# First attention reordered around its score units, and full-width meta scores in the second

## The chip, the cores and the metric

The kernel runs on one core of a Trainium2 chip, as one launch. The metric is the device time of the launch in microseconds. Three timed runs of the kernel before gave a median of 2028.56 us (2028.44 to 2029.75).

## What is computed

Two transformer blocks run one after the other in float32 over 512 tokens of width 1024. The first block prepends 16 meta tokens (528 positions) and has two layers; only its first attention and, in one detail, its second are touched here. The first attention is a differential one, with 8 heads:

```python
def diff_attention(q1, q2, k1, k2, v, lam, ...):
    def probs(qb, k):
        s = einsum('bqhd,bkhd->bhqk', qb, k) * scale          # d = 64
        return softmax(where(mask, s, -inf), axis=-1)
    a = probs(qb1, k1) - lam * probs(qb2, k2)                 # two maps
    return einsum('bhqk,bkhd->bqhd', a, v)                    # v: 128 wide

def diff_attn_layer(h, ...):
    q, k, v = split(rms_norm(h, g_norm) @ w_qkv)              # rotary on q and k
    o = diff_attention(...)
    o = rms_norm(o, g_sub) * (1.0 - lam_init)                 # per head, 128 wide
    return h + o.reshape(B, L, H * DIFF_V_DIM) @ w_o
```

The mask is causal by chunks: the meta tokens are chunk 0, the frames follow in chunks of 64. The second attention (`mla_attention`, 16 heads, 64 + 32 wide) has one map for each head. Gated feed-forward layers, a second block and final norms follow; the diff doesn't touch them.

## The kernel before

Activations lie with features on the partitions and tokens along the free side. A projection is three matmul passes for each 128x128 block (`passes`, L805 to L807): high part by high part, low part of the activation, low part of the weight. DMA brings the weights in halves, ScalarE makes the high part (`hi_part`, L2256), GpSimd the low part (L739). Every engine has one hand-written program in order; semaphores join them.

In the first attention each head is cut into five units. Units 0 to 3 are 128 queries against 528, 400, 272 and 144 keys, unit 4 is the 16 meta queries against 16 keys. For a unit TensorE makes the scores of both maps (`scores`, L1090), VectorE clears a corner (L1806) and takes the negative maximum (L1808, `maximum`), ScalarE the exponentials with their sums (`exps`, L2440), VectorE the combination of both maps (`combine`, L1817 to L1824), TensorE transposes it (`transposes`, L1105 and L1109), ScalarE copies it back (`take_transposed`, L2450 and L2452), TensorE multiplies by the values (`values`, L1121 and L1123) and VectorE copies the output (`take_output`, L1829). The scores of units 1 and above reuse the PSUM banks of unit 0 and so wait for its exponentials.

Between these steps of head h TensorE computes head h+1's query, key and value in six pieces (`piece_a`, 24 passes each) into banks 0 and 1; VectorE takes them out (L1786 for the value). The order on TensorE (`head_a`, L1254): scores of units 1 to 4; for each unit its transposes, one piece, its values; with unit 4 the scores of the next head's unit 0 go ahead. At the end come the sum of squares of head h-1's output (`sub_sum`, L877), also in banks 0 and 1, and the transposes of the next value (`value_transposes`, L1132 and L1133). ScalarE makes the inverse root of that sum (`sub_rms`, `inverse_rms`: logarithm L2324, exponential L2326), VectorE scales head h-2's output and splits it (`sub_scale` L1905, `sub_hi` L1911, `sub_lo` L1916) between the units.

Piece 0 waits until the logarithm has read the sum out of banks 0 and 1: in `piece_a`, L1043, `pe.wait_ge(ln_done, N_SUB + summed + 1)`, with `summed` = hd - 2. Heads 0 and 1 are called with `before=False` and lack that wait; head 0 has `sums=False` and no sum of squares.

The last head (`last_head_a`, L1273) has no next projection. Blocks of the output projection (`wo_blocks`, operands `g_hi` and `g_lo`, eight blocks, one for each head) stand between its units; block k can start when head k's output is normalised and split. `tiles(J_WO, ...)` closes the first two tiles with what is left (`tile_pair`): it waits for block 7 and then runs one block of the first tile and two of the second.

In the second attention `scores_of_b` (L1164) makes one map for each head, in units of the same sizes; its matmuls are L1180, the transposes after them L1190 and L1191. The 16-query unit writes 16 partitions.

## Time and profile before

| | before |
|---|---|
| median of three timed runs | 2028.56 us |
| the profiled execution | 2028.63 us |
| its span | 2026.8 us |
| TensorE matmul busy | 2009.0 us, 99% |
| VectorE busy | 1317.6 us, 65% |
| ScalarE busy | 852.0 us, 42% |
| GpSimd busy | 1164.9 us, 57% |
| first attention, windows from 28 to 251 us | PE busy 216.2 of 223 us |
| mean DMA rate | 90 GB/s |

The profile is of one execution. PE is TensorE's matmul, PEld its weight load, DVE VectorE, ACT ScalarE, POOL GpSimd, SP the DMA-issuing engine. A matmul's duration is modelled, and matmuls overlap, so the distance from one start to the next tells what one costs. A float32 matmul that isn't split into high and low parts shows as two passes. The chain that ended last is followed back from the last instruction to what released each step; the share of an engine in it says how much of the time hangs on that engine. Idle time of another engine costs nothing unless that chain runs over it.

### The profile page before, as it was taken

How to read it: one execution, taken by the hardware profiler on the slowest of the kernel's cores; microseconds unless marked ns; L12 is line 12 of the kernel's file. 1: busy time of each engine (PE TensorE's matmuls, PEld its weight loads, DVE VectorE, ACT ScalarE, POOL GpSimd, SP SyncE). 2: the span in 40 equal slices, each digit the busy share in tenths (PEclk: the TensorE clock that was granted, in tenths of full speed). 3: DMA queues.
4: the chain of work that ended last, by engine and by line, in shares of the span. 5: the costliest groups of instructions: out<-in, count | busy, mean ns of one | idle time of the engine just before them, and what ended most of it. 6: DMA issues, size and time to landing. Idle time of an engine off the chain costs nothing.

```text
span 2026.8 us, 37421 instructions
## 1 busy us (share of the span) xinstructions
PE 2009.0 (99%) x13376; PEld 1804.8 (89%) x13376; DVE 1317.6 (65%) x2199; ACT 852.0 (42%) x1499; POOL 1164.9 (57%) x1395
## 2 busy tenths in 40 slices
PE   9999999999999999999999999999999999999998
PEld 9999899999999988899999998777788888988987
DVE  7777757857746868757857778865512457857654
ACT  5444434433423577634433425344422234433433
POOL 6445356675757522146675767744455557766765
PEclk9999999999999999999999999999999999999999
DMA  5222122232233311122232323322223223232322
GB/s 190 84 74 72 53 85 92 84 117 92 92 97 115 94 34 42 32 89 94 67 131 94 104 94 105 104 84 83 74 93 103 84 84 95 83 125 83 125 83 84
DMA packets 51986, 183.06 MB, mean 90 GB/s; under 512 B 5648, under 2 KB 7824, under 8 KB 51856
## 3 DMA queue, kind: packets, MB, share of 16 engines
q1 hardware_dynamic: 50304, 178.87, 27.3%
q10 hardware_dynamic: 1552, 2.42, 0.4%
q8 instruction: 87, 1.43, 0.3%
q14 instruction: 43, 0.35, 0.1%
HBM read 179.17 MB, written 2.10 MB: 89 GB/s over the span
## 4 chain that ended last, share of the span: by engine, by line
PE 93%; DVE 4%; issue 1%; ACT 1%; POOL 1%; DMA 0%; DVEq 0%; ACTq 0%; SPq 0%
PE ps L805 25%; PE ps L806 24%; PE ps L807 24%; PE ps L929 3%; PE ps L930 3%; PE ps L931 3%; PE ps L1180 2%; PE ps L1197 1%; PE ps L1190 1%; PE ps L1090 1%; PE ps L1121 1%; POOL w_lo L759 1%; PE ps L1105 0%; PE ps L1191 0%; PE ps L1407 0%
## 5 line engine op out<-in xcount | busy, mean ns | idle before, releaser
L739 POOL TENSOR_TENSOR w_lo<-w_raw,w_hi 128x256 fp32r<-128x256 f32 x1140 | 964.1, 878 | 744.5 <-ACT w_hi L2256 735.9
L805 PE MATMUL ps<-x_hi,w_hi 128*128 128x264 f32 (+2 forms) x2504 | 823.0, 329 | 0.0
L806 PE MATMUL ps<-x_lo,w_hi 128*128 128x264 f32 (+2 forms) x2504 | 813.5, 325 | 0.0
L807 PE MATMUL ps<-x_hi,w_lo 128*128 128x264 f32 (+2 forms) x2504 | 812.3, 324 | 0.0
L805 PEld LDWEIGHTS ps<-x_hi,w_hi 128*128 128x128 f32 x2504 | 471.3, 188 | 49.6 <-issue 5.4
L806 PEld LDWEIGHTS ps<-x_lo,w_hi 128*128 128x128 f32 x2504 | 470.8, 188 | 42.1 <-issue 0.2
L807 PEld LDWEIGHTS ps<-x_hi,w_lo 128*128 128x128 f32 x2504 | 471.3, 188 | 39.6
L2256 ACT ACTIVATE w_hi<-w_raw 128x1024 fp32r<-128x1024 f32 x267 | 278.0, 1049 | 72.1 <-PE ps L807 56.4
L805 PE MATMUL ps<-g_hi,w_hi 128*128 128x264 f32 (+3 forms) x648 | 207.9, 321 | 1.0 <-DVE g_lo L1916 1.0
L806 PE MATMUL ps<-g_lo,w_hi 128*128 128x264 f32 (+3 forms) x648 | 205.9, 318 | 0.0
L807 PE MATMUL ps<-g_hi,w_lo 128*128 128x264 f32 (+3 forms) x648 | 205.6, 317 | 0.0
L2393 ACT ACTIVATE scratch<-scratch,par 128x512 f32<-128x512 f32 (+1 forms) x66 | 54.2, 821 | 341.9 <-DVE scratch L1642 341.9
L759 POOL TENSOR_TENSOR w_lo<-w_raw,w_hi 128x256 fp32r<-128x256 f32 x144 | 125.9, 901 | 72.9 <-ACT w_hi L2273 72.6
L805 PEld LDWEIGHTS ps<-g_hi,w_hi 128*128 128x128 f32 x648 | 121.9, 188 | 11.7 <-DVE g_lo L1916 1.4
L806 PEld LDWEIGHTS ps<-g_lo,w_hi 128*128 128x128 f32 x648 | 122.0, 188 | 9.2
L807 PEld LDWEIGHTS ps<-g_hi,w_lo 128*128 128x128 f32 x648 | 122.1, 188 | 8.7
L2190 DVE TENSOR_TENSOR scratch<-ps,acc 128x512 f32<-128x512 f32 x46 | 31.7, 690 | 120.3 <-PE ps L807 120.3
L929 PE MATMUL ps<-g_hi,w_hi 128*128 128x256 f32 (+1 forms) x384 | 108.2, 282 | 0.6 <-DVE h L1568 0.4
L930 PE MATMUL ps<-g_lo,w_hi 128*128 128x256 f32 (+1 forms) x384 | 108.4, 282 | 0.0
L931 PE MATMUL ps<-g_hi,w_lo 128*128 128x256 f32 (+1 forms) x384 | 108.1, 282 | 0.0
L1648 DVE SCALAR_TENSOR_TENSOR scratch<-scratch,par 128x512 f32<-128x512 f32 (+1 forms) x66 | 54.4, 824 | 70.9 <-ACT scratch L2393 70.9
L1656 DVE TENSOR_TENSOR scratch<-ps,r 128x512 f32<-128x512 f32 (+1 forms) x66 | 45.9, 696 | 77.2 <-PE ps L807 76.9
(278 smaller groups left out, 3044.1 us busy)
## 6 DMA issues: line engine op xcount, KB each, us to landing
w_raw<-stream SPq DMA_DIRECT2D x334, 512.0 KB, 3.5
h<-x_t SPq DMA_DIRECT2D x4, 528.0 KB, 6.7
out_t<-h SPq DMA_DIRECT2D x6, 256.0 KB, 2.3
scratch<-rotary_tables ACTq DMA_DIRECT2D x4, 264.0 KB, 5.4
out_t<-h ACTq DMA_DIRECT2D x2, 256.0 KB, 2.5
par<-params ACTq DMA_DIRECT2D x1, 342.0 KB, 4.7
scratch<-positions ACTq DMA_DIRECT2D x1, 256.0 KB, 2.6
cst<-shape_constants ACTq DMA_DIRECT2D x1, 193.0 KB, 6.2
```

What stands on the lines that cost most here:

```text
L739: last = nc.gpsimd.tensor_tensor(w_lo[:, ring(j), cols], w_raw[:, j % 4, cols], w_hi[:, ring(j), cols].bitcast(F32), ALU.subtract)
L759: last = nc.gpsimd.tensor_tensor(chunks_lo[:, slot, cols], src[:, cols], chunks_hi[:, slot, cols].bitcast(F32), ALU.subtract)
L805: nc.tensor.matmul(out_ap, w_hi[:, s, c], xh[:, k, cols], start=first, stop=False)
L806: nc.tensor.matmul(out_ap, w_hi[:, s, c], xl[:, k, cols], start=False, stop=False)
L807: return nc.tensor.matmul(out_ap, w_lo[:, s, c], xh[:, k, cols], start=False, stop=last)
L929: nc.tensor.matmul(out_ap, wh, xh, start=opens and q == 0, stop=False, skip_group_check=True)
L930: nc.tensor.matmul(out_ap, wh, xl, start=False, stop=False, skip_group_check=True)
L931: last = nc.tensor.matmul(out_ap, wl, xh, start=False, stop=q == 3, skip_group_check=True)
L1648: V.scalar_tensor_tensor(conv[:, 0:Tn], a_pad[:, c0 + 1:c0 + 1 + Tn], tap(1), conv[:, 0:Tn], ALU.mult, ALU.add).then_inc(conv_step, 1)
L1656: V.tensor_tensor(cut(b_val[:, 0:Tn], Tn), result(j + 1, Tn), cut(r[:, c0:T], Tn), ALU.mult).then_inc(tile_taken, 1)
L2256: A.activation(w_hi[:, ring(j), :], w_raw[:, j % 4, :], ACT.Copy).then_inc(hi_ready, 1)
L2393: A.activation(conv[:, 0:Tn], a_pad[:, T - Tn:T], ACT.Identity, bias=par[:, bass.ds(b + 2 * i, 1)], scale=par[:, bass.ds(o + 2 * i, 1)]).t ...
```

## The change

- `scores` of units 1 to 4 of head h+1 move from the start of head h+1 to the end of head h, behind its last values. From head 1 on the value transposes follow them and the sum of squares comes last. Head 0 makes the value transposes first. The first head's units 1 to 4 are made ahead of the heads.
- ScalarE: the exponentials of the next head's unit 1 stand behind `take_values` and ahead of `sub_rms`; the other exponentials stand ahead of the take of the unit before.
- VectorE: a unit's combination and piece come ahead of the normalisation step of head h-2.
- The last head is reordered on all three engines. Its sums of squares go to banks 2 and 5 (head 6's) and 4 and 5 (head 7's). `held=1`: the second output tile gets seven blocks before the wait for block 7 instead of six. A pair of banks can be given as a tuple.
- `scores_of_b`: the 16-query unit loads 128 columns of queries and writes all 128 partitions; as before only 16 rows are read.

```diff
@@ norm_sum
+                banks = bank0 if isinstance(bank0, tuple) else (bank0, bank0 + 1)
-                    last = nc.tensor.matmul(ps[:, bank0 + bank, 0:n], ones[:, :], src[:, t0:t0 + n],
+                    last = nc.tensor.matmul(ps[:, banks[bank], 0:n], ones[:, :], src[:, t0:t0 + n],
@@ tile_pair
-                        for b in range(blocks - 1 - m, blocks):
+                        for b in range(blocks - (held if m else 1), blocks):
@@ scores_of_b
-                s = scores_b(idx)
+                s = scores_b(idx) if t else ps[:, 4, UNIT_COLS[2] + UNIT_COLS[3]:UNIT_COLS[2] + UNIT_COLS[3] + META]
-                    last = nc.tensor.matmul(s[:, k0:k1], q_b[rows, h % 4, q0:q0 + nq], k_b[rows, h % 4, k0:k1],
+                    last = nc.tensor.matmul(s[:, k0:k1], q_b[rows, h % 4, q0:q0 + P], k_b[rows, h % 4, k0:k1],
@@ TensorE, head_a
-                for idx in range(1, 5):
-                    step(scores, idx)
                 for idx in range(5):
...
+                if not sums:
+                    value_transposes(hd + 1, 1 - par_)
+                for idx in range(1, 5):
+                    scores(hd + 1, 1 - par_, idx)
                 if sums:
-                    sub_sum(hd - 1, 1 - par_, 0, 6 * hd + 11)
-                value_transposes(hd + 1, 1 - par_)
+                    value_transposes(hd + 1, 1 - par_)
+                    sub_sum(hd - 1, 1 - par_, (0, 1), 6 * hd + 11)
@@ TensorE, last_head_a
-                for idx in range(1, 5):
-                    scores(hd, par_, idx)
                 transposes(hd, par_, 0)
-                sub_sum(HEADS_A - 2, 0)
+                pe.wait_ge(ln_done, N_SUB + HEADS_A - 2)
+                wo_blocks(0, 0, 0, 5)
                 values(hd, par_, 0)
+                pe.wait_ge(exp_done, 5 * hd + 2)
+                sub_sum(HEADS_A - 2, 0, (2, 5))
                 transposes(hd, par_, 1)
-                pe.wait_ge(ln_done, N_SUB + HEADS_A - 1)
-                wo_blocks(0, 0, 0, 5)
+                wo_blocks(0, 1, 0, 5)
                 values(hd, par_, 1)
                 transposes(hd, par_, 2)
-                wo_blocks(0, 1, 0, 5)
+                wo_blocks(0, 0, 5, 6), wo_blocks(0, 1, 5, 6)
                 values(hd, par_, 2)
                 transposes(hd, par_, 3)
-                wo_blocks(0, 0, 5, 6), wo_blocks(0, 1, 5, 6)
+                wo_blocks(0, 0, 6, 7), wo_blocks(0, 1, 6, 7)
                 values(hd, par_, 3)
                 transposes(hd, par_, 4)
-                wo_blocks(0, 0, 6, 7), wo_blocks(0, 1, 6, 7)
+                pe.wait_ge(ln_done, N_SUB + HEADS_A - 1)
+                wo_blocks(1, 0, 0, 2)
                 values(hd, par_, 4)
                 pe.wait_ge(exp_done, 5 * HEADS_A)
                 pe.wait_ge(r_ready, N_SUB + HEADS_A - 1)
-                wo_blocks(1, 0, 0, 3)
-                sub_sum(HEADS_A - 1, 1, 4)
-                wo_blocks(1, 0, 3, 6), wo_blocks(1, 1, 0, 6)
+                wo_blocks(1, 0, 2, 6)
+                sub_sum(HEADS_A - 1, 1, (4, 5))
+                wo_blocks(1, 1, 0, 7), wo_blocks(1, 0, 6, 7)
@@ VectorE, head_a
                 for idx in range(4):
+                    combine(hd, par_, idx + 1)
+                    piece_a(hd + 1, 1 - par_, idx)
                     if norms and idx < 3:
                         (sub_scale, sub_hi, sub_lo)[idx](hd - 2)
-                    combine(hd, par_, idx + 1)
-                    piece_a(hd + 1, 1 - par_, idx)
                     take_output(hd, par_, idx)
@@ VectorE, last_head_a
+                combine(hd, par_, 1)
                 sub_scale(hd - 2)
-                combine(hd, par_, 1)
+                combine(hd, par_, 2)
+                sub_hi(hd - 2), sub_lo(hd - 2)
                 take_output(hd, par_, 0)
-                sub_hi(hd - 2), sub_lo(hd - 2)
-                combine(hd, par_, 2)
+                combine(hd, par_, 3)
+                sub_scale(hd - 1)
                 take_output(hd, par_, 1)
-                sub_scale(hd - 1)
-                combine(hd, par_, 3)
+                sub_hi(hd - 1), sub_lo(hd - 1)
+                combine(hd, par_, 4)
                 take_output(hd, par_, 2)
-                sub_hi(hd - 1)
-                combine(hd, par_, 4)
-                sub_lo(hd - 1)
@@ ScalarE, head_a
                 for idx in range(5):
+                    if idx in range(1, 4):
+                        exps(hd, par_, idx + 1)
+                    take_transposed(hd, par_, idx)
                     if idx == 4:
-                        take_transposed(hd, par_, idx)
                         exps(hd + 1, 1 - par_, 0)
-                    else:
-                        exps(hd, par_, idx + 1)
-                        take_transposed(hd, par_, idx)
...
                 take_values(hd + 1, 1 - par_)
+                exps(hd + 1, 1 - par_, 1)
                 if isinstance(hd, int) and hd == HEADS_A - 2:
                     sub_square(hd, par_)
                 if sums:
@@ ScalarE, last_head_a
-                exps(hd, par_, 1)
                 take_transposed(hd, par_, 0)
-                sub_rms(hd - 1)
-                for idx in range(1, 4):
-                    exps(hd, par_, idx + 1)
-                    take_transposed(hd, par_, idx)
+                exps(hd, par_, 2)
+                sub_rms(hd - 1, (2, 5))
+                take_transposed(hd, par_, 1)
+                exps(hd, par_, 3)
+                take_transposed(hd, par_, 2)
+                exps(hd, par_, 4)
+                take_transposed(hd, par_, 3)
                 take_transposed(hd, par_, 4)
```

## Rows read from the trace of the kernel before

**Rows 1.** The page: its first line, and the chain that ended last by engine

```profile
span 2026.8 us, 37421 instructions
...
PE 93%; DVE 4%; issue 1%; ACT 1%; POOL 1%; DMA 0%; DVEq 0%; ACTq 0%; SPq 0%
```

**Rows 2.** Windows: us, busy PE, PEld, DVE, ACT, POOL, PEclk, DMA share, GB/s

```profile
166.00:194.00 28.00, 27.53 (x224) 25.77 (x222) 21.11 (x55) 13.65 (x38) 13.43 (x17) 1.00 0.24 75
```

**Rows 3.** Waits of PE, 28 to 256 us: total us, times, longest us

```profile
PE ps L1105 <- DVE scratch L1824: 2.8, 6, 0.5
```

**Rows 4.** Timeline of PE, head boundary: start us, us, instruction, [idle before]

```profile
170.33 0.29 PE L1123 MATMUL ps<-scratch 128*128 128x16 f32 x2
170.47 1.26 PE L877 MATMUL ps<-sq,ones 128*128 128x264 f32 x4
...
172.20 1.77 PE L1090 MATMUL ps<-scratch 64*128 64x400 f32 x16
173.91 0.66 PE L1105 MATMUL ps<-cst,scratch 128*128 128x128 f32 x4
...
174.43 0.37 PE L805 MATMUL ps<-x_hi,w_hi 128*128 128x264 f32 x1
...
177.41 1.05 PE L1121 MATMUL ps<-scratch 128*128 128x128 f32 x8
178.31 0.39 PE L1123 MATMUL ps<-scratch 128*128 128x128 f32 x2
179.16 0.55 PE L1105 MATMUL ps<-cst,scratch 128*128 128x128 f32 x3 [0.47 <-DVE scratch L1824]
...
183.27 0.39 PE L1123 MATMUL ps<-scratch 128*128 128x128 f32 x2
183.49 0.38 PE L1105 MATMUL ps<-cst,scratch 128*128 128x128 f32 x2
```

**Rows 5.** Timeline of DVE and ACT, the same boundary

```profile
171.93 1.11 DVE L1824 SCALAR_TENSOR_TENSOR scratch<-scratch,small 128x528 f32<-128x528 f32 x1
...
172.96 0.68 ACT L2324 ACTIVATE acc<-ps,small 128x528 f32<-128x528 f32 x1
...
174.08 0.17 DVE L1806 MEMSET ps<- 64x128 f32 x1 [1.04 <-PE ps L1090]
...
175.31 0.59 ACT L2440 ACTIVATE scratch<-ps,small 128x400 f32<-128x400 f32 x1 [0.99 <-DVE small L1808]
...
176.46 0.59 ACT L2450 ACTIVATE scratch<-ps 128x512 f32<-128x512 f32 x1
...
176.91 0.75 DVE L1905 SCALAR_TENSOR_TENSOR scratch<-scratch,small,acc 128x528 f32 x1
```

**Rows 6.** Timeline of PE and DVE, the last head

```profile
226.20 0.29 PE L1123 MATMUL ps<-scratch 128*128 128x16 f32 x2
...
244.23 0.29 PE L1123 MATMUL ps<-scratch 128*128 128x16 f32 x2
...
245.56 1.13 PE L877 MATMUL ps<-sq,ones 128*128 128x264 f32 x4
...
249.53 1.12 DVE L1916 TENSOR_TENSOR g_lo<-scratch,g_hi 128x528 fp32r<-128x528 f32 x1
...
250.71 0.39 PE L805 MATMUL ps<-g_hi,w_hi 128*128 128x264 f32 x1 [0.75 <-DVE g_lo L1916]
```

**Rows 7.** Second attention: timeline at a meta unit; groups of PEld by form

```profile
748.05 0.55 PE L1180 MATMUL ps<-scratch 128*128 128x144 f32 x4
748.17 0.43 PE L1180 MATMUL ps<-scratch 128*128 128x144 f32 x3
748.38 0.11 PEld L1180 LDWEIGHTS ps<-scratch 128*16 128x16 f32 x2
...
L1180 PEld LDWEIGHTS ps<-scratch 128*128 128x128 f32 x80 | 12.5, 190 | 3.8 <-DVE scratch L1856 2.4 <-issue 0.3
L1180 PEld LDWEIGHTS ps<-scratch 128*16 128x16 f32 x16 | 0.9, 94 | 1.2
```

More of the change, by code:

```diff
@@ L831, in pair_blocks, with tile_pair @@
                            b == 0, False)
-            def tile_pair(j, tl, blocks, xh, xl, T, ready, begun=False):
+            def tile_pair(j, tl, blocks, xh, xl, T, ready, begun=False, held=2):
                 if not begun:
@@ L845, in tile_pair, with tiles @@
                     last.then_inc(half_done, 1)
-            def tiles(j, tl, n, blocks, xh, xl, T, ready, after_first=None, paired=False, begun=False, T_odd=None):
+            def tiles(j, tl, n, blocks, xh, xl, T, ready, after_first=None, paired=False, begun=False, T_odd=None, held=2):
                 done = 0
@@ L855, in tiles @@
                 if paired:
-                    tile_pair(j, tl, blocks, xh, xl, T, ready, begun)
+                    tile_pair(j, tl, blocks, xh, xl, T, ready, begun, held)
                     done = 2
@@ L1244, in head_b, with sub_sum @@
                     output_blocks(1, 1, 0, 6)
-            def sub_sum(n, par_, bank0=0, pieces=0):
+            def sub_sum(n, par_, bank0=(0, 1), pieces=0):
                 pe.wait_ge(r_ready, N_SUB + n)
@@ L1317, in _ @@
             value_transposes(0, 0)
+            for idx in range(1, 5):
+                scores(0, 0, idx)
             head_a(0, 0, sums=False, before=False)
@@ L1325, in _ @@
             last_head_a()
-            tiles(J_WO, TL_WO, KD, KD, g_hi, g_lo, T1, (g_ready, G_WO), paired=True, begun=True)
+            tiles(J_WO, TL_WO, KD, KD, g_hi, g_lo, T1, (g_ready, G_WO), paired=True, begun=True, held=1)
             ffn(J_F0, TL_F0, X_F0, G_F0, T1, N_F0, layer=0)
@@ L2319, in inverse_rms @@
                     act.wait_ge(ss_ready, norm + 1)
-                    src = ps[:, bank0, 0:T2] if T == T2 else ps[:, bank0:bank0 + 2, 0:T // 2]
+                    a, b = bank0 if isinstance(bank0, tuple) else (bank0, bank0 + 1)
+                    src = ps[:, a, 0:T2] if T == T2 else ps[:, a:b + 1:b - a, 0:T // 2]
                 else:
@@ L2460, in sub_square, with sub_rms @@
                 square(o_buf[:, n, :], par_, 0, (o_taken, 5 * n + 5), (ss_ready, N_SUB + n - 1), T1)
-            def sub_rms(n, bank0=0):
+            def sub_rms(n, banks=(0, 1)):
                 wait(act, sub_step, n)
-                inverse_rms(N_SUB + n, P, T1, acc, bank0)
+                inverse_rms(N_SUB + n, P, T1, acc, banks)
             def head_a(hd, par_, j, i=0):
@@ L2612, in _ @@
             take_values(0, 0)
+            exps(0, 0, 1)
             head_a(0, 0, 4)
@@ L2621, in _ @@
             sub_square(HEADS_A - 1, 1)
-            sub_rms(HEADS_A - 1, 4)
+            sub_rms(HEADS_A - 1, (4, 5))
             residual(J_WO, TL_WO, T1, N_F0)
```

## Prediction

> **What bounds the kernel now.** The page comes first: TensorE holds 93% of the chain that ended last, so only what moves a TensorE instruction moves the end [rows 1]. The table of windows gives the stretch that the diff touches: in a window of 28.00 us, about one steady head of the first attention, TensorE is busy 27.53 at full clock (1.00) [rows 2]. So little idle time is left there to return. The list of waits says where: TensorE's transposes (L1105) waited six times for VectorE's combination (L1824), 2.8 us in all [rows 3]. Next the timeline of one head boundary on TensorE [rows 4], beside VectorE and ScalarE in the same stretch [rows 5]. All times below are of that head. I count from V, the start of the last value product of a head (L1123, 170.33), because everything before V is set by TensorE and keeps its order.
>
> TensorE after V, before the change: sum of squares 170.47, value transposes, four score units 172.20 to 173.91, transposes of unit 0, first projection piece P0 at 174.43, values of unit 0 at 177.41, transposes of unit 1 (T1) at 179.16 [rows 4]. After those value passes (178.31) T1 would follow in 0.22, as the next unit's did (183.27 to 183.49) [rows 4], at 178.53; so the wait costs 0.63. From V to T1 is 8.83 us.
>
> The wait arises because VectorE stood idle 1.04 us until the four score units were there (clearing L1806 at 174.08), then did four maxima (to 176.91), then a normalisation step (L1905, 0.75), and only then the combination of unit 1 [rows 5].
>
> **The change, steady heads.** Scores of the next head's units 1 to 4 go straight behind V; value transposes and sum of squares follow. On TensorE this is a permutation of groups. The scores' weight rows are 64 and the rest 128 both before and after, with the same number of changes between them, so I give it 0 (0.1 either way for each boundary in the bounds). TensorE could therefore still reach P0 at 174.3 to 174.4 (perhaps 0.1 earlier, as the sum no longer stands first behind the last piece).
>
> VectorE: combination of unit 0 starts at 171.93 and takes 1.11 [rows 5], ending at 173.04. The scores, 1.71 us long [rows 4], now start about 170.6 and end about 172.4, so even 0.5 us of lateness would be covered. The maxima begin at 173.04 instead of 174.08. They end 2.83 later (174.08 to 176.91) at 175.9, and the combination of unit 1, now ahead of the normalisation, is done 1.5 later (179.16 minus 176.91 minus 0.75) at 177.4. T1 waits for it no more: 0.63 returned, if nothing else is late.
>
> Something else is. ScalarE used to take the logarithm of the sum of squares (L2324) at 172.96, right behind the value copies [rows 5]. The diff puts the exponentials of the next head's unit 1 ahead of `sub_rms`. P0 still begins with a wait on `ln_done` (L1043), because sum and pieces share banks 0 and 1, and the ScalarE queue is in order. So P0 inherits the maximum's chain: clearing at 173.04; exponentials 1.23 later (174.08 to 175.31) at 174.27; these take 1.15 (175.31 to 176.46), to 175.42; the logarithm takes 0.68 [rows 5], to 176.10. P0 starts at 176.1 instead of 174.43, 1.67 later. Behind P0 everything on TensorE is queued: P0 and the values take 2.98 + 0.90 + 0.22 = 4.10 [rows 4], and T1 stands at 180.2 instead of 179.16. **A steady boundary gets 1.0 us longer.** The readiness of unit 1 (177.4) and of the values' operand (two ScalarE steps behind the logarithm, about 177.5 by estimate, against values at 179.1) leaves no second wait. Later units have more than a microsecond of slack, since they follow TensorE's own pieces.
>
> P0 has this wait in heads 2 to 6, five times; heads 0 and 1 are called with `before=False`, and head 0 keeps its old order. Sum: 5 x 1.0 = +5.0. Bounds: 0.7 if VectorE's operations overlap by 0.1 and a release costs nothing, and 1.3 if releases cost 0.05 each and the permutation 0.1. So +3.5 to +6.5.
>
> **The last head** [rows 6]. Before: V at 226.20, last values 244.23, last sum 245.56, low part of the last operand 249.53 + 1.12, and TensorE resumes at 250.71 with 18 passes left before both tiles are closed. After: the five-block group waits for the same late logarithm, with a square of half a microsecond (estimate) now ahead of it, to about V + 6.3 = 232.5. Then the hand chain in V-time is: five blocks (15 passes of 0.122) and the values to 235.5, sum of squares to 236.6, transposes of unit 1 to 237.0, five blocks to 238.9, values to 239.8, transposes and blocks 5 to 240.9. Values of unit 2 wait for the output copy that now follows combination 3 (241.4), and blocks 6 wait for their operand (242.5). Then values 3, transposes 4 and two more blocks to 244.9. The last values are at 244.9, 0.7 later than before; 12 passes instead of 9 stand before the last sum (+0.37), so TensorE resumes at about 251.75, 1.04 later, but with 12 passes left instead of 18 (-0.73). Sum: +0.3, bounds -1.2 and +1.5, because six waits of this chain are estimates from neighbouring durations.
>
> **Wide meta scores** [rows 7]. In the second attention the 16-query unit loads 16 weight columns. Its two 144-column passes follow each other by 0.12 (748.05, 748.17). The second should leave TensorE after the same 0.12, at 748.29, but the 16-wide load starts only at 748.38, so 0.09 to 0.10 of nothing lies between. All 16 heads have such a pair (32 loads of 16). With 128 columns the nearest case is the 16-column pass with a full load in the first attention, which lies 0.14 before the next group (170.33 to 170.47) [rows 4] and shows no such hole. So 0.10 x 16 = -1.5 us. Bounds: 0 if the wide load fills the hole, -2.4 if the following transposes start better too. The Trainium skill (TensorEngine Tiling (Array Packing), Key Properties) says that a change of tiling mode drains TensorE; the hole at the 16-wide load agrees. Against it stands the same skill's "TensorE: Matmul & The Clock Gate", LDWEIGHTS: a load costs time by its columns, P/1.2 ns, which would make each of 32 loads 93 ns longer, an estimate of +3.0 us; no row here shows a 16-column pass with both widths in this place.
>
> The passes themselves, all weights and DMAs stay. `held` only regroups passes. Moved waits on GpSimd's or SP's queue: none; ScalarE's weight conversions keep their places among the units, and so do GpSimd's parts that follow them.
>
> **Sum.** 2028.63 (profiled execution; median 2028.56, the span is 2026.8) + 5.0 + 0.3 - 1.5 = **2032.4 us**.
>
> **Rivals.**
> (a) The logarithm is not late. If unit 1's maximum or its exponentials finish some 1.7 us sooner than my chain, P0 does not wait, T1 loses its wait of 0.63 and the sum its 0.13 behind the last piece: 5 x 0.76 = -3.8, the last head about -1.5, meta -1.5: 2021.8, faster. For it: TensorE's own order is better. Against it: the chain is built from rows of one head, and its deciding instruction, the combination of unit 0 at 171.93, hangs on V. Chance 0.12.
> (b) The wide load costs what it adds: loads of 16 took 94 ns, loads of 128 took 190 [rows 7]; 32 x 96 ns = +3.1 in place of -1.5: 2037.0, slower. It decides where a load is not hidden behind the pass before it, which a 16-column pass can't do. Against it: the full load of 170.33 that shows no hole [rows 4]. Chance 0.08. The load rule of the Trainium skill's page named above would bring about this case.
> (c) The change does little: the logarithm's lateness is smaller (0.5 us for each boundary) and meta gives 1.5: 2028.63 + 2.5 - 1.5 + 0.3 = 2029.9. Chance 0.15.
> (d) The last head's chain slips by more (its outputs copied behind combinations): +2.5 rather than +0.3: 2034.6. Chance 0.1.
> The forecast itself: 0.55, with its own range 2030.5 to 2034.5.
>
> **How the numbers follow.** A measurement of this kernel can tell about 0.2%, 4.1 us, from no change, so 2032.6 is the border. Of the forecast's 0.55 some 0.3 lies below it and 0.25 above; (b) and (d) lie above, (c) below, (a) is faster. Faster 0.12, same 0.45, slower 0.43. The range leaves out (a) and the far end of (b): 2026 to 2036.5.
>
> **What would show it.** In the profile after: P0's first pass in heads 2 to 6 waits for ScalarE's logarithm by about 1.7 us and the transposes L1105 wait for VectorE no more; a steady boundary V to T1 is 9.8 us and a head 28.9; VectorE's 1.04 us of idle before the first clearing are gone; the 16-column pass of the second attention follows its neighbour in 0.12. I am wrong if P0 starts within 4.2 us of V, if the hole at the meta unit stays, or if the last head resumes much later than 25.5 us after its V.

## The result, and the profile after

The changed kernel takes 2036.53 us (median of six runs, 2035.79 to 2039.95) against 2028.5 for the kernel before in the same session (2027.96 to 2029.86): a ratio of 1.0041, 95% interval 1.003 to 1.0051. Run again in another session it took 2037.07 (1.004, 1.0026 to 1.0054). It is slower, by twice the bound of 0.2%. The forecast was 2032.4 with a range up to 2036.5: right in direction, short by 4.1 us, and the range missed. The profiled execution took 2036.26, its span is 2034.5.

The page first, as in [rows 1]: the first line, and the chain that ended last by engine.

```profile
span 2034.5 us, 37425 instructions
...
PE 93%; DVE 3%; ACT 1%; issue 1%; DMA 0%; POOL 0%; DVEq 0%; SPq 0%; ACTq 0%; POOLq 0%
```

7.7 us more of span, and still TensorE. The waits of TensorE between 28 and 265 us (total us, times, longest us) answer to [rows 3]:

```profile
PE ps L805 <- ACT acc L2330: 9.0, 5, 1.9
PE ps L805 <- issue: 1.5, 1, 1.5
PE ps L805 <- DVE g_lo L1922: 1.1, 1, 1.1
```

The six waits of the transposes for VectorE's combination are gone. In their place the first pass of P0 (L805) waits for ScalarE's logarithm (L2330) at all five steady boundaries, and so does the first output block in the last head (also L805). The profile puts five of these six waits down to the logarithm and the one of head 6, 1.5 us, to "issue". Now the boundary that answers to [rows 4 and 5]. TensorE's timeline (start us, us, instruction, idle before):

```profile
176.31 0.29 PE L1124 MATMUL ps<-scratch 128*128 128x16 f32 x2
176.53 1.77 PE L1091 MATMUL ps<-scratch 64*128 64x400 f32 x16
178.23 0.66 PE L1133 MATMUL ps<-cst,scratch 128*128 128x128 f32 x4
...
178.83 1.06 PE L878 MATMUL ps<-sq,ones 128*128 128x264 f32 x4
179.83 0.66 PE L1106 MATMUL ps<-cst,scratch 128*128 128x128 f32 x4
...
182.36 0.38 PE L805 MATMUL ps<-x_hi,w_hi 128*128 128x264 f32 x1 [1.76 <-ACT acc L2330]
...
186.47 0.49 PE L1106 MATMUL ps<-cst,scratch 128*128 128x128 f32 x3
```

VectorE and ScalarE beside it:

```profile
177.91 1.11 DVE L1830 SCALAR_TENSOR_TENSOR scratch<-scratch,small 128x528 f32<-128x528 f32 x1
179.04 0.17 DVE L1812 MEMSET ps<- 64x128 f32 x1
...
182.75 0.63 DVE L1830 SCALAR_TENSOR_TENSOR scratch<-scratch,small 128x400 f32<-128x400 f32 x1
...
180.27 0.59 ACT L2446 ACTIVATE scratch<-ps,small 128x400 f32<-128x400 f32 x1 [0.49 <-DVE small L1814]
...
181.42 0.70 ACT L2330 ACTIVATE acc<-ps,small 128x528 f32<-128x528 f32 x1
```

VectorE goes from the combination straight to the first clearing (its 1.04 us of idle are gone), ScalarE from the exponentials to the logarithm, and TensorE has nothing between 180.59 and 182.36. T1 at 186.47 waits for nothing. From this V (176.31) to the next is 29.11 us, against 27.92 (mean of the five) before.

But not every boundary looks so. Measured from V to V, the five are 30.65, 30.63, 29.12, 29.11 and 28.95 us long: the first two lose another 1.5. The timeline at the first of them, and the windows (us, busy PE, PEld, DVE, ACT, POOL, PEclk, DMA share, GB/s) of both and of a steady head as in [rows 2]:

```profile
91.97 0.39 PE L805 MATMUL ps<-x_hi,w_hi 128*128 128x264 f32 x1 [1.77 <-ACT acc L2330]
92.19 0.28 PE L806 MATMUL ps<-x_lo,w_hi 128*128 128x264 f32 x1
...
92.80 0.41 PE L805 MATMUL ps<-x_hi,w_hi 128*128 128x264 f32 x1
93.01 0.42 PE L806 MATMUL ps<-x_lo,w_hi 128*128 128x264 f32 x1
93.23 0.42 PE L807 MATMUL ps<-x_hi,w_lo 128*128 128x264 f32 x1
...
93.00:96.20 3.20, 3.20 (x16) 3.20 (x16) 0.00 (x0) 2.44 (x7) 1.53 (x3) 0.50 0.15 56
123.30:127.00 3.70, 3.70 (x20) 3.70 (x19) 0.34 (x1) 2.78 (x8) 1.68 (x3) 0.54 0.22 89
147.00:176.00 29.00, 27.24 (x223) 25.65 (x223) 21.72 (x55) 13.56 (x39) 13.40 (x16) 1.00 0.23 72
```

TensorE resumes at 91.97 after 2.0 us without a new pass. The passes behind the first start 0.12 apart, and from 92.80 on they stand 0.22 apart: the granted clock is at the lower level (0.50 of 2.4 GHz) until about 96.2. Below I call this a fall of the clock. P0 takes 4.54 us instead of 3.0. The same idle at 180.59 to 182.36 leaves the clock at 1.00.

Where the 7.7 us of span came from, by the same events in both traces:

| stretch | before | after | difference |
|---|---|---|---|
| start to the first head's V | 59.76 | 59.10 | -0.7 |
| from there to the last head's V: 26.81 without a change, then the five boundaries | 166.44 | 175.26 | +8.8 |
| last head, V to the sum of squares behind attention | 67.89 | 68.74 | +0.85 |
| to the second attention | 424.39 | 424.45 | +0.1 |
| second attention | 145.11 | 144.29 | -0.8 |
| what follows it | 1155.99 | 1155.40 | -0.6 |

The first line, the fourth and the last hold some scatter: other executions of programs that are equal there give 59.1 to 60.0 at the start, 423.9 to 425.1 up to the second attention and 1155.4 to 1156.1 at the end.

### The profile page after: what moved, and what is told of

Read it like the earlier page. It is cut to its first block, busy times and chain, and to the rows that moved or that the text cites. A ratio compares the mean times of both kernels' runs of the same rounds, so it can differ in the third digit from the quotient of the medians.

```text
span 2034.5 us, 37425 instructions
## 1 busy us (share of the span) xinstructions
PE 2008.8 (99%) x13376; PEld 1807.9 (89%) x13376; DVE 1317.8 (65%) x2199; ACT 852.0 (42%) x1499; POOL 1164.7 (57%) x1395
## 3 DMA queue, kind: packets, MB, share of 16 engines
q8 instruction: 87, 1.43, 0.3%
## 4 chain that ended last, share of the span: by engine, by line
PE 93%; DVE 3%; ACT 1%; issue 1%; DMA 0%; POOL 0%; DVEq 0%; SPq 0%; ACTq 0%; POOLq 0%
PE ps L805 25%; PE ps L806 24%; PE ps L807 24%; PE ps L930 4%; PE ps L931 4%; PE ps L932 4%; PE ps L1181 1%; PE ps L1198 1%; PE ps L1122 1%; PE ps L1191 1%; PE ps L1091 1%; DVE small L1845 1%; DMA w_raw<-stream 0%; ACT scratch L2540 0%; PE ps L1413 0%
## 5 line engine op out<-in xcount | busy, mean ns | idle before, releaser
L805 PE MATMUL ps<-x_hi,w_hi 128*128 128x264 f32 (+2 forms) x2504 | 824.5, 329 | 8.6 <-ACT acc L2330 7.0
L805 PEld LDWEIGHTS ps<-x_hi,w_hi 128*128 128x128 f32 x2504 | 472.8, 189 | 59.6 <-issue 15.0
L805 PE MATMUL ps<-g_hi,w_hi 128*128 128x264 f32 (+3 forms) x648 | 208.1, 321 | 3.3 <-ACT acc L2330 1.9
L805 PEld LDWEIGHTS ps<-g_hi,w_hi 128*128 128x128 f32 x648 | 122.0, 188 | 14.4 <-ACT acc L2330 2.2
```

The lines of the kernel that those rows point to most:

```text
L805: nc.tensor.matmul(out_ap, w_hi[:, s, c], xh[:, k, cols], start=first, stop=False)
```

## Experiments

**The logarithm first.** The changed kernel, but ScalarE takes the logarithm before the exponentials of the next head's unit 1.

```diff
                 take_values(hd + 1, 1 - par_)
+                if sums:
+                    sub_rms(hd - 1)
                 exps(hd + 1, 1 - par_, 1)
                 ...
                     sub_square(hd, par_)
-                if sums:
-                    sub_rms(hd - 1)
```

> The changed kernel with one ScalarE edit: the inverse root of the sum of squares stands ahead of the exponentials of the next head's unit 1. Theory (the logarithm is late because those exponentials stand ahead of it on ScalarE's in-order queue): the sum ends 3.6 us after V, so the logarithm can begin at V + 3.7 and P0 starts at V + 4.6 instead of V + 6.05; the exponentials move behind it and T1 stands at about V + 8.7; a steady head takes 27.8 us instead of 29.1 or 30.6, no piece runs at half clock, and the time is 2027 to 2028.5 us. Rival (P0 is held by something else, such as the order of the groups on TensorE or the value copies): P0 stays near V + 6 and the time near 2036.5.

2026.1 us (ten runs; ratio 0.9985, 0.9975 to 0.9995). Its boundary on TensorE:

```profile
172.19 1.06 PE L878 MATMUL ps<-sq,ones 128*128 128x264 f32 x4
...
174.28 0.38 PE L805 MATMUL ps<-x_hi,w_hi 128*128 128x264 f32 x1 [0.33 <-ACT acc L2330]
```

and on ScalarE:

```profile
173.34 0.70 ACT L2330 ACTIVATE acc<-ps,small 128x528 f32<-128x528 f32 x1 [0.21 <-PE ps L878]
```

The wait of P0 falls from 1.76 to 0.33, heads are 27.6 to 27.7 us long (27.53 for the last), and the clock stays at 1.00. One line of ScalarE's order turns the slower kernel into one slightly faster than before, by 10.4 us. So the late logarithm is the cause of the loss, in both its forms (the idle, and the clock after it). TensorE's new order isn't free, though. V of this boundary is at 169.66, and the sum of squares, now the last group, starts at V + 2.53 instead of V + 0.14. The logarithm waits 0.21 for it, and P0 starts at V + 4.62 where the kernel before has V + 4.10. Some 0.4 to 0.5 us for each boundary stays lost: the five boundaries take 138.2 us here, against 136.05 in the kernel with VectorE's order alone (below).

**Filling the idle.** The changed kernel with seven matmuls of ones by ones, used by nobody, ahead of unit 0's transposes, where TensorE would otherwise stand still; nothing is left out.

```diff
-            def transposes(hd, turn, idx):
+            def transposes(hd, turn, idx, fill=0):
                 ...
+                for _ in range(fill):
+                    nc.tensor.matmul(ps[:, 7, 2 * P:3 * P], ones[:, :], ones[:, :], start=True, stop=True)
                 ...
-                    step(transposes, idx)
+                    transposes(hd, par_, idx, 7 if before and idx == 0 else 0)
```

> The changed kernel, with seven more matmuls of ones by ones (14 passes, 1.5 us, into unused columns of bank 7) ahead of the transposes of unit 0 in each head that waits for the logarithm. They add no result and take no wait away; they only make TensorE's idle time before P0 0.5 instead of 2.0 us. Theory (the two heads of 30.6 us are heads in which the clock fell to 0.50 after 2.0 us of idle): the clock falls nowhere, all pieces take 3.0 us, P0 still starts at V + 6.05, steady heads are all 29.1 us, and the time is about 2033.4 us. Rival (the slow stretches come from the load of the whole chip or from late weights, not from the idle time before them): two heads stay at 30.6 and the time at 2036.5 or above.

```profile
90.46 1.83 PE L1106 MATMUL ps<-ones 128*128 128x128 f32 x14
92.13 0.60 PE L1108 MATMUL ps<-cst,scratch 128*128 128x128 f32 x4
...
93.00 0.38 PE L805 MATMUL ps<-x_hi,w_hi 128*128 128x264 f32 x1 [0.16 <-issue]
...
93.00:97.00 4.00, 4.00 (x33) 4.00 (x34) 1.69 (x5) 3.47 (x9) 1.29 (x2) 1.00 0.33 123
```

The first three lines are TensorE's timeline at the first boundary, the last is a window behind P0. P0 comes no earlier (V + 6.06), but the clock stays at 1.00 and all heads are 29.1 to 29.2 us (28.96 the last): the stretch of the heads is 172.29 instead of 175.26, 3.0 us shorter. That much is the clock. Yet the whole kernel takes 2036.58, as much as without the filling. By the stretches of the table, against the first trace of the changed kernel: 1.0 more at the start and 0.75 less up to the second attention, both little more than scatter, and 2.95 more behind the second attention. There most of the 3 us is given back.

**Half the filling,** three matmuls in place of seven:

```diff
-                    transposes(hd, par_, idx, 7 if before and idx == 0 else 0)
+                    transposes(hd, par_, idx, 3 if before and idx == 0 else 0)
```

> As the filled wait, with three matmuls of ones by ones (6 passes, 0.66 us) in place of seven: no result and no wait changes, TensorE's idle time before P0 is 1.4 instead of 2.0 us. The seven fillings took both slow stretches out of the first attention (172.3 us from the first V to the last, against 175.3), yet the whole time stayed at 2036.6, with stretches of 1 to 2 us lost at the start, near 1250 us and near 1900 us. Theory (those later losses are the scatter of single executions or follow where the code lies, and the clock is worth 1.5 us for each fall): the attention stretch is again 172.3 and the time lies between 2033 and 2036. Rival (what the filling gives is always given back later): 2036.5.

TensorE now goes 1.3 us without a new pass (1.0 at head 6). There is no fall of the clock either, the heads take the same 172.29, and the time is again 2036.3 (five runs, ratio 1.0035, 1.0021 to 1.0048).

**Both again,** the changed kernel and the one with seven filling matmuls, in one session (no edits).

> The changed kernel as it is, beside the filled wait on one chip. Theory (falls of the clock behind 2 us of idle cost about 1.5 us each and come in every execution): its granted clock is 0.996 to 0.998, its time 7.5 to 9 us above the kernel before, and 1.5 to 3.5 us above the filled wait run beside it. Rival (the filling's gain is given back): both have one time.

> The filled wait once more (seven matmuls of ones by ones, nothing else), beside the changed kernel. Theory: granted clock 0.998 or 0.999, time 5.5 to 6.5 us above the kernel before, since the late logarithm (5.9 us from the first V to the last) stays. Rival: the time of the changed kernel.

2037.07 and 2036.31 (ratios 1.004 and 1.0036, intervals overlapping almost wholly). The second trace of the changed kernel has one fall in place of two, at another boundary: heads 29.11, 29.11, 29.11, 30.66, 28.98. So for one and the same program the clock falls in some executions of a boundary and not in others, while P0 starts at the same V + 6.05 in each of the first four.

```profile
122.00:126.00 4.00, 4.00 (x35) 4.00 (x35) 1.70 (x6) 3.29 (x9) 1.47 (x3) 1.00 0.28 109
180.50:184.50 4.00, 4.00 (x23) 4.00 (x22) 0.56 (x1) 3.00 (x8) 1.76 (x3) 0.57 0.27 104
```

These are two windows of that trace, behind P0 of the second and of the fourth boundary: 35 passes in 4 us at 1.00, 23 at 0.57.

Where the filled kernels give their gain back shows in the list of waits from 880 us to the end. First the changed kernel, complete; then the one with seven filling matmuls:

```profile
PE ps L967 <- ACT sq L2363: 0.5, 1, 0.5
```

```profile
PE ps L930 <- ACT sq L2288: 1.8, 2, 1.3
PE ps L967 <- ACT sq L2365: 0.5, 1, 0.5
PE ps L930 <- DVE h L1576: 0.4, 1, 0.4
```

The 1.3 us stand at 1906 us, far from anything that was edited. ScalarE, which converts the weights there, waited for their transfer. In the filled kernel, then in the changed one:

```profile
1906.46 0.63 ACT L2280 ACTIVATE w_hi<-w_raw 128x512 fp32r<-128x512 f32 x1 [3.80 <-DMA w_raw<-stream]
```

```profile
1906.11 0.63 ACT L2278 ACTIVATE w_hi<-w_raw 128x512 fp32r<-128x512 f32 x1 [2.17 <-DMA w_raw<-stream]
```

And the DMA of that stretch in the filled kernel, 1901 to 1908 us in 40 slices (busy share in tenths, GB/s), with the queues:

```profile
DMA  0000009417996997999999953010000000100000
GB/s 0 0 0 0 0 0 304 70 70 281 328 257 257 374 421 304 398 445 445 374 374 445 375 234 94 23 23 0 23 23 23 23 23 23 47 0 0 0 0 0
...
q8 instruction: 1, 0.02, 0.9%
...
w_raw<-stream SPq DMA_DIRECT2D x2, 512.0 KB, 5.7
```

After the bulk of the two transfers, 23 GB/s trickle on for 1.6 us, which I read as one DMA engine that is behind the others. A packet of the instruction queue q8 starts at 1904.3, inside the transfers. In the changed kernel it starts at 1906.5, near their end (1907.0), and they land in 4.0 us instead of 5.7. The three traces of filled kernels all have such a wait of 1.2 to 1.5 us near 1906 (two of them others besides): what follows the second attention lasts 1158.35, 1158.72 and, with the half filling, 1156.84 us, against 1155.40 and 1155.37 in the two traces of the changed kernel. The suspicion is that more TensorE instructions shift the loads of its program against the weight transfers.

**Filling at the start only,** and **filling at both places.** The warm-up ahead of all work is made of 50 small matmuls instead of 15, 70 passes more, in the changed kernel (first) and in the one with seven filling matmuls (second). These passes are slow (100 of them took 21.5 us), and the passes behind them still run at half pace: the first eight take 3.87 us where the changed kernel has 2.05. So both kernels end their first head 18.3 us later; nothing is left out.

```diff
-                for _ in range(15):
-                    nc.tensor.matmul(ps[:, 5, 0:P], ones[:, :], ones[:, :], start=True, stop=True)
+                for _ in range(50):
+                    nc.tensor.matmul(ps[:, 5, 0:P // 4], ones[:, :], ones[:, 0:P // 4], start=True, stop=True)
```

> The changed kernel, with the warm-up at the very start made of 50 small matmuls (32 columns) in place of 15 of 128 columns: 35 matmuls, 70 passes more in TensorE's program and nothing added anywhere else. The question is why the kernels with 15 or 35 filling matmuls at the boundaries gain 3 us in the first attention and lose 1.4 to 3 us at the end: there a piece waits 1.2 to 1.5 us for a weight transfer whose last packets trickle on one of the 16 DMA engines, and a packet of the instruction queue lies inside that transfer, while in the changed kernel it lies behind it. Theory A, a longer program shifts the instruction loads against the weight transfers: this kernel shows the same waits at a piece near 1906 us (and perhaps near 1152), the rest after the second attention is 1157 to 1158.4 us in place of 1155.4, and the boundaries still show 29.1 or 30.6. Time about 2038 to 2040. Theory B, the waits came from the filling of the boundaries or of the heads themselves: rest 1155.4, no wait for ScalarE near 1906, time about 2036.5, plus or minus what the other warm-up costs at the start.

> The kernel with seven filling matmuls at each of the five boundaries, with the same longer warm-up: 70 matmuls more than the changed kernel, twice the shift. No boundary should lose the clock (29.1 each). Theory A: the instruction packet moves again, by as much as before; if it leaves the transfer near 1906 the wait there goes, the rest is 1155.4 to 1157, and the time about 2033.5, the 3 us of the clock now seen in the whole; if it meets another transfer the wait appears elsewhere. Theory B: the rest stays at 1158.4 and the wait near 1906 stays where it was.

2057.18 and 2051.49 us. The waits from 880 us to the end, of the first and, complete, of the second:

```profile
PE ps L930 <- ACT sq L2286: 1.6, 2, 1.2
PE ps L967 <- ACT sq L2363: 0.5, 1, 0.5
PE ps L930 <- DVE h L1574: 0.4, 1, 0.4
```

```profile
PE ps L967 <- ACT sq L2365: 0.5, 1, 0.5
```

With 70 passes more at the start and none at the boundaries, the late weights are back (1.2 us at 1799, others near 1179 and 1044) and what follows the second attention lasts 1158.15, like that of the filled kernels. With 140 passes more they are gone, and it lasts 1155.53. So the wait goes with how many passes TensorE's program has before that point, wherever they stand and whatever they do. One trace each shows this for the two kernels here, two for the seven filling matmuls. That the instruction packet is its carrier is my reading and not shown: in all four traces with such a wait near 1906 or 1799 a packet of q8 starts inside the late transfers, in both traces of the changed kernel near their end. What puts one DMA engine behind wasn't isolated. The Trainium skill ("Runtime: NRT & Kernel Launch", Instruction fetch mechanics) says that each engine's sequencer fetches its program over its own DMA queue in blocks of 16 KiB, and calls this fetch hidden. The 87 packets and 1.43 MB of q8 in the changed kernel's page agree with the size; whether the fetch is what delays the weights, no run here shows.

The second kernel also settles the clock in the whole time. Less the 18.3 us of its start it is 2033.2, 3.3 below the changed kernel: with the late weights out of the way, the 3 us of the clock show. The first has three falls (boundaries 29.12, 30.67, 30.65, 30.66, 28.98), and the two differ by 5.7 us in time, by 6.9 in span: 4.6 in the heads, 2.6 behind the second attention.

**The last head as before.** The changed kernel with the kernel before's `last_head_a` on TensorE, VectorE and ScalarE, and `held` at 2. In short:

```diff
                 transposes(hd, par_, 0)
-                pe.wait_ge(ln_done, N_SUB + HEADS_A - 2)
-                wo_blocks(0, 0, 0, 5)
+                sub_sum(HEADS_A - 2, 0, (0, 1))
                 values(hd, par_, 0)
...
-                combine(hd, par_, 1)
                 sub_scale(hd - 2)
-                combine(hd, par_, 2)
-                sub_hi(hd - 2), sub_lo(hd - 2)
+                combine(hd, par_, 1)
```

> The changed kernel with the last head in the order of before on all three engines, and two blocks of the second tile held back as before. It keeps the late logarithm of head 5. From the last V to the first feed-forward sum of squares the kernel before took 67.9 us and the changed one 68.7. Theory (the new last head returns about what the late logarithm costs it): here the stretch is 69 to 70 us, because the old order puts the sum of squares of head 6 first and so waits for the same logarithm's exponential. Rival (the new order itself costs the 0.8): 67.9.

One run, 2040.37; its trace has three falls of the clock at the boundaries (29.11, 30.66, 30.63, 30.67, 28.95). The last head is 69.83 us long, against 68.74 with the new order and 67.89 before the change. But it holds a fourth fall, which no trace with the new last head has. These are the windows over it and behind it:

```profile
244.90:248.30 3.40, 3.40 (x18) 3.40 (x18) 2.28 (x6) 2.73 (x8) 0.00 (x0) 0.50 0.00 0
248.30:252.00 3.70, 3.70 (x33) 3.70 (x33) 2.34 (x9) 1.72 (x11) 0.00 (x0) 1.00 0.00 0
```

It stands behind a wait of 2.61 us of the sum of squares. The groups in that window took some 1.7 us more than the same groups of the changed kernel's last head (an estimate from the distances of their starts), which is more than the 1.1 by which the two orders differ. So what the new order of the last head is worth by itself isn't shown; this one run only shows that the old order had the longer wait.

**The wide meta scores alone.** The kernel before, with 128 weight columns in place of 16:

```diff
-                s = scores_b(idx)
+                s = scores_b(idx) if t else ps[:, 4, UNIT_COLS[2] + UNIT_COLS[3]:UNIT_COLS[2] + UNIT_COLS[3] + META]
                 ...
-                    last = nc.tensor.matmul(s[:, k0:k1], q_b[rows, h % 4, q0:q0 + nq], k_b[rows, h % 4, k0:k1],
+                    last = nc.tensor.matmul(s[:, k0:k1], q_b[rows, h % 4, q0:q0 + P], k_b[rows, h % 4, k0:k1],
```

> The kernel before with the full-width meta scores of the second attention alone. Theory (a 16-wide load leaves 0.09 us of nothing before it and a load of 128 does not): the 16-column pass follows its neighbour in 0.12 instead of 0.216, the stretch of the second attention is 0.8 us shorter, and the time is 2027.7. Rival (a full load costs its columns): 32 x 0.096 = 3.1 us more, 2031.6.

2027.73 (ten runs, ratio 0.9997, 0.9987 to 1.0006): the difference from the kernel before is within the noise. In the trace the second attention is 144.29 us, 0.82 shorter.

**VectorE's order alone.** The kernel before, with the combination and the next piece ahead of the normalisation step in `head_a`:

```diff
                 for idx in range(4):
-                    if norms and idx < 3:
-                        (sub_scale, sub_hi, sub_lo)[idx](hd - 2)
                     combine(hd, par_, idx + 1)
                     piece_a(hd + 1, 1 - par_, idx)
+                    if norms and idx < 3:
+                        (sub_scale, sub_hi, sub_lo)[idx](hd - 2)
```

> The kernel before with one VectorE edit of the change alone: in the steady heads a unit's combination and the taking of a piece stand ahead of the normalisation step. Theory (T1 waited 0.63 us for a combination that stood behind a step of 0.68): T1's wait falls to nothing, a steady head takes 27.3 instead of 27.9, and the time is 2025.4. Rival (the wait is only moved, to P1, to the next transposes or to the scores of the next head): heads stay at 27.9 and the time at 2028.5.

2025.04 (ten runs, ratio 0.9981, 0.9972 to 0.9991). A window of 28 us in its steady heads, to be held against [rows 2]:

```profile
166.00:194.00 28.00, 28.00 (x230) 26.53 (x230) 22.09 (x56) 14.13 (x39) 13.47 (x16) 1.00 0.25 80
```

TensorE is busy for all of it. Heads are 27.2 us, 0.7 shorter, and 5 x 0.72 = 3.6 is what the time shows (3.5). This one edit takes the whole of T1's wait; the new order of TensorE, which was also to take it, isn't needed, and it costs the 0.4 to 0.5 us for each boundary told above.

**VectorE's order in every head, with meta.** As the one before, plus `combine(hd, par_, 1)` ahead of `sub_scale(hd - 2)` in the last head, plus the wide meta scores.

```diff
-                sub_scale(hd - 2)
                 combine(hd, par_, 1)
+                sub_scale(hd - 2)
                 take_output(hd, par_, 0)
```

> The kernel before with three edits of the change: combinations and pieces ahead of the normalisation steps in the steady heads, in the last head combination 1 ahead of the first normalisation step, and full-width meta scores. Theory: the gains of the two parts add up, -3.5 and -0.8, and the last head gives up to 0.5: 2024 us, faster than both kernels. Rival (the last head's swap delays the blocks it feeds and takes back what it gave): 2025 or above.

2025.01 (eleven runs, ratio 0.9981, 0.9972 to 0.999). The heads are as short, but the last one is 68.53 instead of 67.90: there the swap costs 0.6, which is about what meta gives.

**The best of both.** VectorE's order in `head_a` (the diff of VectorE's order alone) and the wide meta scores (both edits of the diff of meta alone), the last head as before.

> The kernel before with two edits of the change: combinations and pieces ahead of the normalisation steps in the steady heads, and full-width meta scores; the last head as before. Theory (the swap in the last head of the version with three edits cost it 0.6): stretch from the last V to the feed-forward sum 67.9 again, 3.5 and 0.8 us taken from the time before, and 2024.3 us. Rival (the two parts don't add up): 2025 or above.

2024.37 (2023.24 to 2025.69, eleven runs; ratio 0.9976, 0.9967 to 0.9985), span 2021.4. It beats both kernels. A head of 27.2 us has no idle time on TensorE:

```profile
168.00:195.20 27.20, 27.20 (x224) 25.73 (x223) 21.99 (x55) 13.53 (x39) 13.48 (x16) 1.00 0.24 77
```

## Why the prediction was right, and where it was wrong

**The chain was right, nearly to the hundredth.** From V (176.31): the clearing at V + 2.73 (predicted 2.71), the exponentials at 3.96 (3.94), the logarithm at 5.11 and ended at 5.81 (5.77), the combination of unit 1 done at 7.07 (7.1), P0 and the values 4.11 (4.10), no second wait. VectorE's idle and T1's wait went as said. Rival (a), that the logarithm isn't late, is out, and the run with the logarithm first shows that it is the cause. That run shows too that rival (a) was priced too well: with a prompt logarithm the five boundaries are 1.4 us shorter than before, not 3.8, because the logarithm still has to wait for the sum of squares, which the new order puts last.

**The release was counted at nothing.** P0 starts at V + 6.05, 0.24 after the logarithm's end; the kernel with the logarithm first has the same 0.24 (it ends at 174.04, P0 is at 174.28). My upper bound held 0.05 for a release. That much it was only in the last head; at head 6 it was 0.10, and why the four boundaries before it have 0.24 is open. A steady boundary became 1.16 to 1.20 longer where the clock held (1.04 for head 6), not 1.0: five of them +5.8 in place of +5.0, still inside the bounds of 3.5 to 6.5.

**The failed step: "a steady boundary gets 1.0 us longer", five times.** It took the passes behind the wait at their durations from a trace in which TensorE never stood still that long. After the new idle the clock fell in two of five boundaries, 1.5 us each, so the five cost +8.8. No term and no bound had this; it alone, 3.0 us, is the larger part of the miss of 4.1, and it puts the time beyond the range. The direction doesn't hang on it: without the two falls the boundaries still cost 5.8. That TensorE would stand still for some 2 us was in my own sum; what followed it was not asked. The other misses, +0.8 for the release, +0.55 in the last head and +0.7 in the second attention, are partly hidden in the total by -1.3 at the start and the end, which is luck.

**The last head** gave +0.85 against +0.3 (bounds -1.2 to +1.5). Its first group waited 1.93 for the logarithm and started at V + 6.40 (predicted 6.3), its last values are at V + 18.9 (predicted 18.7), and TensorE resumes at V + 25.65, 1.14 later than before (predicted 1.04):

```profile
234.36 0.29 PE L1124 MATMUL ps<-scratch 128*128 128x16 f32 x2
...
240.76 0.39 PE L805 MATMUL ps<-g_hi,w_hi 128*128 128x264 f32 x1 [1.93 <-ACT acc L2330]
...
249.79 0.68 PE L1122 MATMUL ps<-scratch 128*128 128x128 f32 x4 [0.66 <-DVE scratch L1835]
...
260.01 0.39 PE L805 MATMUL ps<-g_hi,w_hi 128*128 128x264 f32 x1 [1.09 <-DVE g_lo L1922]
```

The chain of six estimates held to 0.2; what fell short is the gain behind it, from having 12 passes left instead of 18: 0.3 instead of 0.73. Rival (d), +2.5, is out.

**The meta scores** gave -0.8 against -1.5. The hole did go. Before, four passes and then the transposes stood 0.48 apart (748.05 [rows 7] to 748.53); after:

```profile
773.57 0.54 PE L1181 MATMUL ps<-scratch 128*128 128x144 f32 x4
773.95 0.41 PE L1191 MATMUL ps<-cst,scratch 128*128 128x128 f32 x2
```

0.38, so 0.10 less for each head, as predicted. But the second attention as a whole shortened by half of 16 x 0.10, because half of the heads kept their length. The trace of the meta scores alone shows where the rest went. Its list of waits in the second attention has

```profile
PE ps L1197 <- ACT scratch L2532: 1.7, 7, 0.4
```

and the kernel before has the same wait once, with 0.3 us: the value products (L1197) now wait for ScalarE's exponentials (L2532), which I hadn't looked for. Rival (b), that the wide load costs what it adds, is out, since the second attention got shorter, not longer.

The rule of the Trainium skill ("TensorE: Matmul & The Clock Gate", LDWEIGHTS) says that a load costs time by its columns. The loads themselves did become longer (190 ns in place of 94), but taken as a cost of the whole it would have made an estimated +3.0, and the second attention with the meta scores alone measured -0.8. The Trainium skill ("TensorEngine Tiling (Array Packing)", Key Properties) says that a change of tiling mode drains TensorE. The hole that went agrees with this; no run here separates a drain from another cause.

**The sum, corrected:** 2028.63 + 5.8 (boundaries) + 3.0 (clock) + 0.85 - 0.8 = 2037.5, against 2036.26 measured in the profiled execution; the 1.2 left over are the start and the end of the kernel (-0.7 and -0.6 in the table), where TensorE has the same instructions as before and other executions scatter by as much.

**What stays open.** Why the clock falls behind some of the equal idles: two of five boundaries, one of five, three of five and three of five in four traces. The boundary of head 6, where TensorE goes 1.7 us without a new pass, never had a fall; of the sixteen others, with 2.0 us, nine had one. What TensorE did before them is the same each time as far as the rows show. The length of the idle doesn't decide alone either: in the last head 2.2 us without a new pass had no fall in seven traces. I can only give the price of a fall, and that filling the idle, wholly or in part, avoided all of them in four traces (twenty boundaries, sixteen of them of the kind that fell).

## What to carry to other kernels

Moving work ahead in one in-order queue moves everything behind it: look for the instruction in that queue that the bounding engine waits for. Here a single logarithm behind two exponentials cost 10 us, and one swap on VectorE takes the whole wait that the large reorder was meant to take. Moving a group to the end of TensorE's order delays whatever follows from it as well. When a sum puts a new idle of some microseconds on TensorE, the passes behind it may run at half clock: keep an upper bound for each such place. And a control that adds instructions can change the time somewhere else through the length of the program alone, so compare it by stretches, not by its total.

## What the chip showed that I had not expected

- After 2.0 us without a new pass, TensorE's granted clock fell from 1.00 to 0.50 at some boundaries. It fell after the passes had resumed, 0.8 to 0.9 us after in both traces of the changed kernel and 0.1 to 0.3 us after in the kernels with the longer start and the old last head, and it stayed there for about 3.4 us. A fall cost 1.5 us either way (P0 4.53 to 4.56 instead of 3.0).
- From the end of ScalarE's logarithm to the first pass that waits for it are 0.24 us at the boundaries of heads 2 to 5, 0.10 at head 6 and 0.05 in the last head of the changed kernel. The first two are the same with the logarithm first.
- With 70 more passes in TensorE's program, at the boundaries or at the start, two weight transfers hundreds of microseconds later landed in 5.6 to 5.7 instead of 4.0 us, and what follows the second attention took 2.6 to 3.3 us more; 140 more passes cost nothing there.
- The 16-column pass behind a 16-wide load starts 0.22 us after the pass before it, behind a 128-wide load 0.12, though [rows 7] have the wide loads twice as long (190 against 94 ns).
